# Input projection and gates of a hybrid decoder block in split precision, softmax division on ScalarE

## The reference, cut to what matters

```python
h      = rms_norm(x) * (1 + scale) + shift            # shift, scale, gate from silu(c) @ ada_w + ada_b
proj   = h @ w_in                                     # 2048 x 7536, parts:
q_nsa, kv_nsa, g_nsa, c_q, c_kv, k_r, g_merge = parts  # 1024, 1536, 48, 512, 256, 32, 4096 columns
o_nsa  = native sparse attention of q_nsa, kv_nsa     # 16 heads; compressed + selected + window branch
o_mla  = latent attention of c_q, c_kv, k_r           # 16 heads, after two up-projections
merged = sigmoid(g0) * (o_nsa @ w_nsa) + sigmoid(g1) * (o_mla @ w_mla)
x1     = x + gate * rms_norm(merged @ w_out)
out    = x1 + gate * rms_norm(PEER(x1))               # 8 heads pick 16 of 16384 experts per token
```

## Time and profile before

| | us |
|---|---|
| median of 3 runs | 2361.51 |
| lowest and highest | 2361.07, 2363.28 |
| the profiled execution: its own time | 2363.7 |
| its span from first to last instruction | 2362.0 |

### The profile page before, as it was taken

The page is one execution under the profiler, slowest core; times in us unless marked ns, Lnnn a source line. Parts: engine busy times, 40 slices in busy tenths (PEclk is TensorE's granted clock), DMA queues, the critical chain, the costliest instruction groups (busy, mean ns, idle before and its releaser), DMA issues.

```text
span 2362.0 us, 17146 instructions
## 1 busy us (share of the span) xinstructions
PE 1963.9 (83%) x5571; PEld 1005.8 (43%) x5571; DVE 1306.1 (55%) x2208; ACT 439.3 (19%) x995; POOL 721.9 (31%) x656
## 2 busy tenths in 40 slices
PE   1789999999999999988887788778678777778786
PEld 0245564444456777873333333333233333333332
DVE  6756224664265647576555555555475555555553
ACT  0001011222234544331011101110211111111101
POOL 2112000000000000024654554355336544653560
PEclk9889889999999999998989888889888988988897
DMA  9978636776564564469999999999999999999996
GB/s 343 366 263 329 209 105 210 254 264 224 161 244 172 194 237 150 143 256 421 411 404 412 422 412 420 416 423 417 415 409 408 414 416 422 420 421 420 422 413 259
DMA packets 161483, 774.93 MB, mean 328 GB/s; under 512 B 15028, under 2 KB 21352, under 8 KB 86036
## 3 DMA queue, kind: packets, MB, share of 16 engines
q0 software_dynamic: 91648, 637.57, 66.7%
q1 hardware_dynamic: 67684, 132.80, 16.1%
q10 hardware_dynamic: 2096, 3.85, 0.4%
HBM read 772.04 MB, written 2.13 MB: 328 GB/s over the span
## 4 chain that ended last, share of the span: by engine, by line
PE 42%; DMA 31%; DVE 10%; issue 8%; POOL 7%; ACT 1%; DVEq 0%; POOLq 0%; ACTq 0%; SPq 0%
DMA arena<-in_peer_u_dram,idx_now 26%; PE PS L874 14%; PE PS L1264 11%; POOL arena L525 7%; DMA arena<-in_ada_w_dram 2%; PE PS L867 2%; PE PS L1251 2%; PE PS L868 2%; PE PS L869 2%; PE PS L915 1%; DVE arena L1382 1%; PE PS L1047 1%; DVE arena L1773 1%; DVE arena L1328 1%; DMA w_raw<-in_peer_w_q_dram 1%
## 5 line engine op out<-in xcount | busy, mean ns | idle before, releaser
L1264 PE MATMUL PS<-arena 128*128 128x512 f32 x2048 | 1011.9, 658 | 268.1 <-ACT arena L826 268.1
L1773 DVE CUSTOM_DVE_ANT_0 arena<-arena 128x2048 f32<-128x2048 f32 x256 | 586.2, 2293 | 480.3 <-DMA arena<-in_peer_u_dram,idx_now 479.8
L1264 PEld LDWEIGHTS PS<-arena 128*128 128x128 f32 x2048 | 428.2, 212 | 851.1 <-issue 546.9
L525 POOL DMA_INDIRECT arena<-in_peer_v_dram,idx_now x256 | 323.5, 1264 | 276.6 <-PE PS L1264 186.0
L874 PE MATMUL PS<-arena 128*128 128x512 f32 (+1 forms) x912 | 406.6, 591 | 0.0
L525 POOL DMA_INDIRECT arena<-in_peer_u_dram,idx_now x256 | 321.6, 1256 | 111.8 <-issue 72.5
L874 PEld LDWEIGHTS PS<-arena 128*128 128x128 f32 x912 | 168.0, 192 | 174.3 <-issue 167.7
L820 ACT ACTIVATE act_g<-dots 128x4 f32<-128x4 f32 x64 | 13.1, 205 | 946.8 <-DVE dots L1773 946.8
L461 POOL DMA_DIRECT2D arena<-in_ada_w_dram x64 | 33.8, 529 | 485.8 <-DVE arena L1382 274.4
L1585 DVE TENSOR_TENSOR w_lo<-w_raw,w_hi 128x1024 fp32r<-128x1024 f32 x96 | 116.0, 1223 | 108.2 <-ACT w_hi L710 107.7
L511 POOL COPY idx_now<-idx_next 128x16 uint32<-128x16 uint32 x16 | 3.7, 229 | 560.3 <-DVE idx_next L1754 560.3
(11 more groups left out here) (259 smaller groups left out, 1650.4 us busy)
## 6 DMA issues: line engine op xcount, KB each, us to landing
arena<-in_ada_w_dram POOLq DMA_DIRECT2D x96, 1024.0 KB, 5.7
arena<-in_w_in_dram SPq DMA_DIRECT2D x112, 512.0 KB, 5.6
w_raw<-in_w_out_dram SPq DMA_DIRECT2D x32, 512.0 KB, 3.6
w_raw<-in_peer_w_q_dram SPq DMA_DIRECT2D x32, 512.0 KB, 3.5
w_raw<-in_w_branch_nsa_dram SPq DMA_DIRECT2D x16, 512.0 KB, 4.2
w_raw<-in_w_branch_mla_dram SPq DMA_DIRECT2D x16, 512.0 KB, 3.5
arena<-in_x_dram SPq DMA_DIRECT2D x4, 1024.0 KB, 6.6
arena<-in_cmp_w_dram SPq DMA_DIRECT2D x8, 512.0 KB, 10.7
```

The source lines that it names most:

```text
L525: pool.indirect_dma_start(ring[e % RING], None, tab, bass.IndirectOffsetOnAxis(ap=idx_now[:, now, e:e + 1], axis=0)).then_inc(landed[e % R ...
L1264: ins = nc.tensor.matmul(PS[:, bank + k, :], diag[e % 8], Vrow[e % RING][:, k * NC:(k + 1) * NC], start=(first and e == 0), stop=False, sk ...
L1773: v.tensor_tensor_reduce(row, row, h2[:, t, :], 1.0, 0.0, ALU.mult, ALU.add, dots[:, e:e + 1]).then_inc(u_free, 1)
```

## The change

1. **Split operands for the whole input projection and the gates.** `products` calls `split_product` with `hT_hi`, `hT_lo` and `w_hi`, `w_lo`. The compression MLP and the two up-projections stay as they were (`is_split` is false for their tiles). All tiles use the ring of four, so SP loads tile m once tile m-4 has been used; before, eight slots.
2. **hT in two parts.** After PE turned a bank, ACT rounds it to `hT_hi` and DVE subtracts to `hT_lo`, for both token tiles; before, ACT copied one and DVE the other. PE may reuse a bank once `hT_lo` is made.
3. **Where the casts stand.** `high_to(m)` on ACT and `low_to(m)` on DVE bring all split tiles up to m, in the order of the code. They stand between the other work of those engines; in the attention loops one tile per unit, on ACT behind the exp, on DVE between `mask_max` and the reciprocal.
4. **The division.** DVE only makes the reciprocals (and multiplies the branch gate in); ACT scales the probabilities in `normalise`. `ada_row` moves behind the reciprocals.
5. **The attention result** is copied out of PSUM as float32 (`oT`, ACT), which frees the bank at once, and is split later, four pairs at a time (`heads_high` on ACT, `heads_low` on DVE).
6. **Order elsewhere.** The angles move to the start of DVE's work, with their wait for `small_in`; the sines stand ahead of ACT's first casts. The third `rope` moves behind the compression input, and the `ada_row` calls are spread anew (2, 3, 7, 2, 2 instead of 8, 4, 2, 2). DVE's latent norm moves behind the compressed branch's softmax. Some buffers move in SBUF.

```diff
-WSLOTS = 8
+SPLIT = 4
...
+        def is_split(m):
+            return not (W_CMP <= m < W_C4 or W_QUP <= m < W_G5)
...
             def load(m, src, cols=NC):
-                if m >= WSLOTS:
-                    sp.wait_ge(w_used, m - WSLOTS + 1)
-                sp.dma_start(wring[:, m % WSLOTS, :, 0:cols], src).then_inc(w_landed[m % WSLOTS], 16)
+                if m >= SPLIT:
+                    sp.wait_ge(w_used, m - SPLIT + 1)
+                sp.dma_start(w_raw[:, m % SPLIT, :, 0:cols], src).then_inc(w_landed[m % SPLIT], 16)
...
+            act.wait_ge(angle_ready, 1)
+            nc.scalar.activation(sincos[:, 0, :, :], ang[:, 0, :], ACT.Sin).then_inc(sin_ready, 1)
+            nc.scalar.activation(sincos[:, 1, :, :], ang[:, 1, :], ACT.Sin).then_inc(sin_ready, 1)
+            for q in range(QTRS):
+                high_to(4 * q + 3)
+                for t in range(NT):
+                    act.wait_ge(tr_done, 2 * q + t + 1)
+                    nc.scalar.copy(hT_hi[:, 4 * q:4 * q + 4, t * P:(t + 1) * P],
+                                   PS[:, 4 + (2 * q + t) % 4, :].rearrange("p (a b) -> p a b", b=P)).then_inc(h_hi, 1)
...
             for k in range(CH_FIRST):
+                high_to(17 + k)
                 main_out(k, CH_FIRST * 8 - 2 * (1 - k))
...
+            high_to(W_C2 + 8 + 2)
             main_out(2, W_C2 + 8)
...
+            def normalise(n):
+                act.wait_ge(srec_ready, n + 1)
+                for t in range(NT):
+                    lo, hi = (0, P) if t == 0 else (P, 3 * P)
+                    ins = nc.scalar.activation(s_prob[:, n % 2, lo:hi], s_prob[:, n % 2, lo:hi], ACT.Copy,
+                                               scale=srec[:, n % 2, t:t + 1])
+                ins.then_inc(prob_ready, 1)
...
                 if n < NSA_UNITS:
                     softmax_exp(n, NSA_SCALE)
+                    high_to(gate_tile(1) + n + 3)
...
                     probs_out(n - 1)
+                if n < NSA_UNITS:
+                    normalise(n)
...
             def products(bank, m, w, k, cols=NC):
                 kk = 2 * w + k
                 for t in range(NT):
+                    rows = slice(t * P, (t + 1) * P)
+                    ins = split_product(PS[:, bank + t, 0:cols], hT_hi[:, kk, rows], hT_lo[:, kk, rows],
+                                        w_hi[:, m % SPLIT, k, 0:cols], w_lo[:, m % SPLIT, k, 0:cols],
+                                        start=(kk == 0), stop=(kk == KD - 1))
...
+            dve.wait_ge(small_in, 16 * 3)
+            link(v.tensor_copy(pos_f[:, :], pos_i[:, :]))
...
             dve.wait_ge(x_in, 16 * NT)
...
                     if q and n == 8 * q:
-                        bank_out(2 * q - 1, hT[:, 4 * q - 4:4 * q, P:2 * P])
+                        hT_low(2 * q - 2)
+                        hT_low(2 * q - 1)
+                    if n % 8 == 5:
+                        low_to(4 * q + 1)
+                    if n % 8 == 7:
+                        low_to(4 * q + 3)
...
                 if n < NSA_UNITS:
                     mask_max(n, NSA_SCALE)
+                    low_to(gate_tile(1) + n + 3)
+                    sums_inverse(n, gnsa[:, :, 3 * (n // 2) + n % 2 + 1])
                     ada_row(KD + n)
-                    normalise(n, gnsa[:, :, 3 * (n // 2) + n % 2 + 1])
...
+            low_to(gate_tile(5) + 8 + 2)
+            for n in range(HEADS):
+                mask_max(NSA_UNITS + n, MLA_SCALE)
+                low_to(gate_tile(6) + n + 3)
+                sums_inverse(NSA_UNITS + n)
+                ada_row(KD + NSA_UNITS + n)
+            for k in range(3):
+                heads_low(k)
+            low_to(W_BR + AHEAD - 1)
+            heads_low(3)
             mod_out(3)
```

More of the change, by code:

```diff
@@ L881, in chunk @@
                     for k in range(2):
-                        ins = products(bank, m + w, w, k, lhs, ktiles, cols)
+                        kk = 2 * w + k
+                        for t in range(NT):
+                            ins = nc.tensor.matmul(PS[:, bank + t, :], lhs[:, kk, t * P:(t + 1) * P],
+                                                   w_raw[:, (m + w) % SPLIT, k, :], start=(kk == 0), stop=(kk == ktiles - 1))
                     ins.then_inc(w_used, 1)
@@ L1405, in rope @@
                     link(ins) if t == 0 else ins.then_inc(done, 1)
+            for r in range(2):
+                ada_row(r)
+            low_to(16)
             dve.wait_ge(sin_ready, 2)
@@ L1409, in _ @@
             rope(KV0, GROUPS, rope_ready)
-            for r in range(8):
-                ada_row(r)
+            low_to(17)
             dve.wait_ge(pj_out, 2)
@@ L1414, in _ @@
             rope(KV0 + 2 * GROUPS * HD, GROUPS, rope_ready)
-            dve.wait_ge(pj_out, 3)
-            dve.wait_ge(rope_ready, 2)
-            rope(KV0 + 4 * GROUPS * HD, GROUPS, rope_ready)
+            low_to(19)
+            for r in range(2, 5):
+                ada_row(r)
+                low_to(17 + 2 * r)
+            low_to(26)
             for b in range(4):
@@ L1549, in mod_out @@
                                        op0=ALU.add, op1=ALU.mult).then_inc(mod_ready, 1)
-            for n in range(NSA_UNITS + 3):
-                if n % 16 == 0 and n < NSA_UNITS:
+            for n in range(NSA_UNITS):
+                if n % 16 == 0:
                     mod_out(n // 16)
@@ L1570, in _, with heads_low @@
             dve.wait_ge(qm_roped, 1)
-            for n in range(HEADS + 3):
-                if n < HEADS:
-                    mask_max(NSA_UNITS + n, MLA_SCALE)
-                    ada_row(KD + NSA_UNITS + n)
-                    normalise(NSA_UNITS + n)
-                if n >= 4 and n % 2 == 0:
-                    pair_low(PAIRS + (n - 4) // 2)
+            def heads_low(k):
+                dve.wait_ge(o_hi, k + 1)
+                part = slice(4 * k, 4 * k + 4)
+                v.tensor_tensor(oT_lo[:, part, :], oT[:, part, :], oT_hi[:, part, :].bitcast(F32), ALU.subtract).then_inc(
+                    o_lo, 1)
+            low_to(gate_tile(5) + 8 + 2)
[8 more added lines that the diff above has]
+            heads_low(3)
             mod_out(3)
-            def w_low(m):
-                dve.wait_ge(hi_ready, m - W_BR + 1)
-                v.tensor_tensor(w_lo[:, m % SPLIT, :, :], w_raw[:, m % SPLIT, :, :],
-                                w_hi[:, m % SPLIT, :, :].bitcast(F32), ALU.subtract).then_inc(lo_ready, 1)
             def merged_low(c_):
@@ L1594, in merged_low @@
                                     mergedT_hi[:, 4 * c_:4 * c_ + 4, cols].bitcast(F32), ALU.subtract).then_inc(mtr_lo, 1)
-            for m in range(AHEAD):
-                w_low(W_BR + m)
             for c_ in range(4):
```

335 lines of the change are left out of this document (186 added, 149 removed).

## The result

| | us |
|---|---|
| kernel before, median of 4 runs | 2362.40 |
| changed kernel, median of 4 runs | 2403.57 (2398.73 to 2408.12) |
| ratio | 1.0173, 95% interval 1.0156 to 1.0190 |
| forecast | 2375 (2353 to 2392) |

The profiled execution of the changed kernel has a span of 2406.4 us, 44.4 more than before; it took 2408.12 us by its own time, the longest of the four.

The account below looks back on a forecast made before the run. It took the projection and both attention loops to wait for PE's matmuls. Terms +9 - 21 + 14 + 2.5 + 7.4 + 2 = +14 take the span from 2362.0 to 2376, or 2375 us against the median; range 2353 to 2392.

Parts of the forecast that it names:

- The first loop: First attention loop: mask_max, exp, cast, subtraction, reciprocal and row form one chain, 6.55 us a unit against 6.00; +14 us.
- The second: Second attention loop: the same chain without the gate, 6.36 us a unit against 5.8; +7.4 us.
- The tail, the up-projections, gate chunk 5: Up-projections and gate chunk 5 together +2.5 us; the second loop's tail, to the branches, +2 us.
- The late start: First stage: angles wait for positions, so DVE begins the adaLN sums at about 29.4 us instead of 17.43, 12 us late.
- C2: Projection chunk right after the first stage: -0.8 us instead of -5.9, since casts and subtractions stand behind DMA issues.
- the first stage's: Start to 165.2 us: late adaLN sums, subtractions in later quarters and bank emptying; +9 us (2 to 14).
- The second term: From the first stage's end to the first attention loop: less PE work, partly given back; -21 us (-38 to -12).
- MLP and C4: Compression MLP -2 us; chunk C4 0, its gain lost to adaLN rows beside the tiles.
- Tiles at PE's pace: Rival, 165 to 377 us: four slots feed PE, that stretch gives -38 to -40; 2353 us, chance 0.16.
- No late start: Rival, first stage: positions land early, the stage costs 0 to +2 us; 2367 us, chance 0.12.
- Loops PE bound: Rival, both attention loops: units stay PE bound at 5 us, 70 us off; 2305 us, chance 0.05.
- The clock falls in the loops: Rival, attention loops: PE idling lowers its clock, units of 8 us or more, +70 us; 2445 us, chance 0.07.

Follow-up runs that it names:

- cast early: Changed kernel with ACT's cast of the attention loops' tiles ahead of the exp and one tile less far ahead; 2349.02 us, 0.9933 of the kernel before.
- the best order that was tried: "cast early" plus angles in quarter 1, later quarter subtractions, third rope in its old place and adaLN rows 5 to 15 spread between subtractions; 2328.86 us, 0.9857.

## Why the prediction was wrong in its size

**Right.** The sign, and the chain in the loops. *The first loop*: "DVE is in line: 6.55 us a unit" was measured as 6.55 in its regular units. *The second*: 6.36 forecast, 6.34 in its regular units. Opening that chain in either of two places made the units 0.5 to 1.3 us shorter, so it was the cause. *The tail, the up-projections, gate chunk 5*: within 0.6 us. *The late start*: the angles at the start of DVE cost 11 to 12.6 us at C2, by the run that moved them to quarter 1 (against the mean of the five starts and against the changed kernel's own).

**The step that failed** is the first stage's, "Each later quarter gets two subtractions that nothing hides (2.4 us) and one more bank to empty (0.7), and the other two lie under PE's column sums. Quarters 1 and 2 had DMA waits of that size, quarter 3 had none: -2, +0.5, +3". Measured: +2.2, +4.4 and +8.9, or 15.4 us where I had 1.5. Two things were wrong in it. DVE's idle time was not a reserve: it waited for slabs whose slots it frees itself, so work put into its line moved the transfers along with it; the doubled subtractions show that, at some 0.7 us for each. And the subtraction of tile 4q+1 waits for a tile that SP may only ask for once PE has used the one four before it (76.83 us in quarter 1, cast at 85.48), with slabs behind it in DVE's order; moving the subtractions took 4 to 6 us off the three quarters. What the two share of the 15.4 us is not settled further. I had also put quarter 0 at +7.6; it was +10.3. The last stretch, to C2, gave back 1.7 us where I had put +0.1. Together 15 of the 30 us.

**The second term**, C2 to the first loop, was -12.7 instead of -21, near the end that I had named, "-12 if each burst of adaLN rows costs one latency more". (Its items add up to -21.8, and for the -38 at PE's pace it shows no working: its own "33 us at PE's pace" is what the items start from.) Piece by piece: C2 +2.6 instead of -0.8, PE waiting 1.37 and 2.82 us for subtractions and at a lower clock behind the second; C3 -5.7, C5 -5.4 and the tail -3.3, all as forecast; MLP and C4 together -0.6 instead of -2; and, from the tail's end to the loop -0.3 where gate chunk 0 and the edges were to give -4.4. In that last stretch PE waits 5.34 us for ACT's copy of qT (4.15 before) and 4.30 us ahead of the loop for the last DVE copy (1.09 before), each behind a cast or a subtraction. For the MLP and C4 the sum came out near by luck: the MLP gave 10.8 us, not 2, and C4 lost 10.2, not 0. The burst of rows that I had named for C4 was the cause there, but PE waited 14 us for it and not 6; moved ahead, it cost the MLP as much, and spreading it gave 5 to 6 us.

**The loops' rest**, 5.2 and 1.8 us. In the first loop 4.2 of it lie in the units: five of the 31 distances were 7.5 us. Three of these are units 10, 14 and 22, in which PE waited 2.5 us for ACT's copy of a finished pair, the fourth is unit 23 behind one; over all four the granted clock was 0.65 to 0.70, and for once mask_max waited for PE, 3.8 us in all; the fifth had a cast that waited 0.81 us for its tile. The forecast had no wait of PE for ACT in the loop at all: it had the scalings done before "PE wants the result", and PE waited for them too, 6.5 us in seven places. That I gave the clock no share inside the forecast, only a rival of its own, was too sharp.

**The rivals.** Tiles at PE's pace: no, PE waited 14 us at C4 alone. No late start: no, 24.05 us. Loops PE bound: not in this order of the code, but at once when the cast stands ahead of exp. The clock falls in the loops: in part, 0.91 and 0.92 granted instead of 1.00, worth some 4 us in the first loop and not 70, because at 6.55 us a unit DVE's chain hides most of a slower PE. The Trainium skill's rule ("TensorE: Matmul & The Clock Gate", HAM oscillation), by which gaps between bursts put the clock down again and again, is borne out at the six waits of 2.0 to 2.5 us for `pair_out`, and not at the shorter ones: 18 of the 31 units kept the full clock. In "cast early", without those waits, all but the first did.

What the split products (with the division on ACT) are worth here: 22 us of the first loop's 196.6 once its chain is open. The whole change, in the best order that was tried, gives 1.4% where its first form took 1.7%.

## What to carry to other kernels

When work is added to an engine that is in line with its own transfers, its idle time is not free: look at who lets the next transfer start. In a loop, write down for each unit what stands between one engine's result and the next one's start; a cast placed ahead of the exp instead of behind it was worth 55 us here. And an edit that goes around one wait can make the next one: compare the starts of the stages, not only the total.
